# Stick-breaking attention cells: the order of the next cell's scores and logarithms against this cell's sums and weights

## The reference, cut to what matters

```python
h = rms_norm(x, norm_mix_g); proj = h @ w_in          # 1024 tokens, 7 x 1024 columns
z = einsum('bhqd,bhkd->bhqk', q, k) / sqrt(64)         # 16 heads
causal = key_pos < q_pos
log_1m = where(causal, -softplus(z), 0)
after = cumsum(log_1m, reverse=True) - log_1m          # over the keys behind this one
w = where(causal, exp(log_sigmoid(z) + after), 0)
o = w @ v
```

## Time and profile before

| what | value |
|---|---|
| time, median of 3 runs | 4964.03 us (4961.4 to 4964.75) |
| the profiled execution | 4961.57 us, of which its span 4959.8 us |
| PE busy | 4612.5 us, 93% |
| DVE busy | 2884.2 us, 58% |
| ACT busy | 1703.9 us, 34% |
| POOL busy | 1781.3 us, 36% |
| granted TensorE clock, mean | 0.964 of full |
| mixer phase | from the start to 1159.0 us |

### The profile page before, as it was taken

One profiled execution on the slowest core, in us unless ns is written; L12 is line 12 of the kernel. 1 busy time (PEld: TensorE's weight loads), 2 busy tenths in 40 slices (PEclk: granted clock), 3 DMA queues, 4 the chain that ended last, 5 costly groups with the idle time before them and its releaser, 6 DMA issues. The chain is left out here.

```text
span 4959.8 us, 62173 instructions
## 1 busy us (share of the span) xinstructions
PE 4612.5 (93%) x21768; PEld 3671.5 (74%) x21768; DVE 2884.2 (58%) x4467; ACT 1703.9 (34%) x2690; POOL 1781.3 (36%) x1078
## 2 busy tenths in 40 slices
PE   6999999986896987999999998999799999999998
PEld 5666666653676765888888887888688888888886
DVE  3777777776425217777777746776344444444445
ACT  3555555553524313333333333444112111111212
POOL 1443433341124115777777761111122222222221
PEclk9999999987998998999999999999899999999999
DMA  2111111103423131222222224555744444444441
GB/s 78 35 47 48 47 44 43 47 18 128 153 97 132 34 127 69 99 97 93 98 97 93 104 106 144 205 204 210 275 149 134 148 145 144 144 148 145 138 144 68
DMA packets 260002, 555.58 MB, mean 112 GB/s; under 512 B 17104, under 2 KB 148432, under 8 KB 246736
## 3 DMA queue, kind: packets, MB, share of 16 engines
q1 hardware_dynamic: 255184, 485.85, 29.1%
q10 hardware_dynamic: 4608, 67.11, 3.3%
HBM read 384.08 MB, written 168.82 MB: 111 GB/s over the span
## 5 line engine op out<-in xcount | busy, mean ns | idle before, releaser
L155 PE MATMUL expert_o<-expert_ahi,expert_vhi 128*128 128x512 f32 x2048 | 799.5, 390 | 25.8 <-POOL expert_vlo L2338 20.8
L156 PE MATMUL expert_o<-expert_alo,expert_vhi 128*128 128x512 f32 x2048 | 798.5, 390 | 0.0
L157 PE MATMUL expert_o<-expert_ahi,expert_vlo 128*128 128x512 f32 x2048 | 798.3, 390 | 0.0
L2402 DVE TENSOR_TENSOR expert_acc<-expert_acc,expert_o 128x512 f32<-128x512 f32 x496 | 341.0, 688 | 709.8 <-PE expert_o L157 704.7
L2338 POOL TENSOR_TENSOR expert_vlo<-expert_vraw,expert_vhi 128x1024 fp32r<-128x1024 f32 x128 | 323.3, 2526 | 1055.8 <-ACT expert_vhi L2356 1055.8
L155 PEld LDWEIGHTS expert_o<-expert_ahi,expert_vhi 128*128 128x128 f32 x2048 | 385.4, 188 | 108.1 <-issue 27.2
L156 PEld LDWEIGHTS expert_o<-expert_alo,expert_vhi 128*128 128x128 f32 x2048 | 385.5, 188 | 80.2 <-issue 0.2
L157 PEld LDWEIGHTS expert_o<-expert_ahi,expert_vlo 128*128 128x128 f32 x2048 | 385.5, 188 | 80.2
L155 PE MATMUL mix_gemm<-mix_hhi,mix_w_hi 128*128 128x512 f32 x896 | 373.8, 417 | 20.5 <-POOL mix_w_lo L185 13.5
L2362 ACT ACTIVATE expert_ahi<-expert_act 128x1024 fp32r<-128x1024 f32 x128 | 135.8, 1061 | 730.2 <-DVE expert_act L2392 730.2
L556 DVE SCALAR_TENSOR_TENSOR mix_room<-mix_u,mix_cwj,mix_room 128x1024 f32<-128x1024 f32 x240 | 361.3, 1505 | 6.1 <-DVE mix_u L528 3.2
(11 more groups left out here) (319 smaller groups left out, 9983.4 us busy)
## 6 DMA issues: line engine op xcount, KB each, us to landing
gates<-spread_stage ACTq DMA_DIRECT2D x32, 2048.0 KB, 15.0
expert_act<-gelu_u SPq DMA_DIRECT2D x128, 512.0 KB, 3.4
expert_graw<-gates SPq DMA_DIRECT2D x128, 512.0 KB, 4.6
expert_vraw<-in_peer_v SPq DMA_DIRECT2D x128, 512.0 KB, 6.5
select_raw<-in_select_pairs SPq DMA_DIRECT2D x54, 1024.0 KB, 5.0
gelu_u<-front SPq DMA_DIRECT2D x184, 256.0 KB, 2.0
mix_w_raw<-in_w_mix SPq DMA_DIRECT2D x56, 512.0 KB, 3.7
spread_uraw<-in_peer_u SPq DMA_DIRECT2D x36, 512.0 KB, 4.8
```

The source lines that it names most:

```text
L155: nc.tensor.matmul(out, whi, xhi, start=(first and i == 0), stop=False)
L156: nc.tensor.matmul(out, whi, xlo, start=False, stop=False)
L157: mm = nc.tensor.matmul(out, wlo, xhi, start=False, stop=(last and i == len(terms) - 1))
L2402: nc.vector.tensor_tensor(acc[:, k, h * H:h * H + H], acc[:, k, h * H:h * H + H], ops[:, d, h], ALU.add).then_inc(added, 1)
```

## The change

Three queues of the attention cells are put in another order; no arithmetic is added or taken away.

- ACT: the six instructions of the logarithms become the helper `log_part`. Those of cell 0 of the first pair are issued ahead of the loop; inside cell i the logarithms of cell i + 1 (in cell 11, those of cell 0 of the next pair) stand behind the high part and the evictions of cell i and ahead of its weight.
- PE: the scores of cell i + 1 stand ahead of `add_own`(i).
- DVE: both log sigmoids stand ahead of the low part of head 1; each log sigmoid gets a wait for the log weight of the cell before.

```diff
+            def log_part(n, a):
+
+                for s in range(2):
+                    act.wait_ge(z_done[s], n + 1)
+                    nc.scalar.activation(expz[:, s, a:H], zps[:, s, a:H], ACT.Abs).then_inc(act_step[s], 1)
+                for s in range(2):
+                    act.wait_ge(act_step[s], n * 2 + 1)
+                    act.wait_ge(ls_done[s], n + 1)
+                    nc.scalar.activation(expz[:, s, a:H], expz[:, s, a:H], ACT.Exp, scale=-1.0).then_inc(act_step[s], 1)
+                for s in range(2):
+                    act.wait_ge(act_step[s], n * 2 + 2)
+                    nc.scalar.activation(ln[:, s, a:H], expz[:, s, a:H], ACT.Ln, bias=1.0).then_inc(ln_done[s], 1)
+
+            log_part(0, col0[0])
+
             def body(j, par, jj, more):
                 for i in range(NCELL):
                     a, n = col0[i], NCELL * j + i
-
-                    for s in range(2):
-                        act.wait_ge(z_done[s], n + 1)
-                        nc.scalar.activation(expz[:, s, a:H], zps[:, s, a:H], ACT.Abs).then_inc(act_step[s], 1)
...
                     for s in range(2):
                         act.wait_ge(sp_done[s], n + 1)
                         act.wait_ge(sp_used[s], n + 1)
@@ -480,6 +484,8 @@
                     if more and i:
                         for g in ends[i - 1]:
                             evict(*following(j, par, jj), g, more)
+                    if more or i < NCELL - 1:
+                        log_part(n + 1, col0[(i + 1) % NCELL])
                     for s in range(2):
                         act.wait_ge(lw_done[s], n + 1 + 1)
                         act.wait_ge(pv_done[s], n + 1)
@@ -571,11 +577,11 @@
                                                              in1=ln[:, s, a:H], op0=ALU.max, op1=ALU.add)
                         ins.then_inc(sp_raw[s] if masked[i] else sp_done[s], 1)
                     for s in range(2):
+                        dve.wait_ge(lw_done[s], n + 1)
                         nc.vector.scalar_tensor_tensor(out=ls[:, s, a:H], in0=zps[:, s, a:H], scalar=0.0,
                                                        in1=ln[:, s, a:H], op0=ALU.min, op1=ALU.subtract
                                                        ).then_inc(ls_done[s], 1)
-                        if s == 0:
-                            low_part(dve, nc.vector, j, 1, i)
+                    low_part(dve, nc.vector, j, 1, i)
@@ -679,12 +685,12 @@
                 for i in range(NCELL):
                     for s in range(2):
-                        add_own(j, s, i)
-                    for s in range(2):
                         if i < NCELL - 1:
                             z_cell(j, par, s, i + 1)
                         elif more:
                             z_cell(j + 1, 1 - par, s, 0)
+                    for s in range(2):
+                        add_own(j, s, i)
```

## The result

The changed kernel takes 4900.12 us (median, 4897.5 to 4906.8), the kernel before beside it 4962.72 us: a ratio of 0.9877, 95% interval 0.986 to 0.9894. That is 61 us less by the ratio, 63 us by the two medians. The forecast was 4936.6 us with a range of 4922 to 4952: the sign was right, but the gain was more than twice the 27.4 us of the forecast, and the time lies outside the range.

A forecast was written before the change was run, and what follows sets the result against it. PE bounds the first seven pairs, a cell's chain, mostly on DVE, the last. 16.2 + 0.9 + 1.7 (into the last pair) + 7.0 - 1.4 + 3.0 = 27.4 us saved: 4936.6 us, range 4922 to 4952.

The forecast's parts named there:

- The changes of pairs: From cell 11 to the next cell 0, the projection starts 2.7 us earlier; six changes give 16.2 us.
- the clock's 3.0: Behind changes of pairs, less half-rate time on PE: 3.0 us, a quarter of the 12 us possible.
- rival (a): At shortened changes of pairs the clock stays up: 12 instead of 3 us, 4928 us in all; chance 15%.
- The start: At the start of the first pair only the scores gain, 0.9 us, as POOL is at a weight chunk.
- The last pair: Cells of the last pair lose DVE waits for logarithm and high part: 7.0 us saved, bounds 0 and 11.6.
- DVE's new wait for the sums: In the last pair, DVE's log weight waits for sums now behind the next scores: 0.3 to 1.1 us.
- Inside the seven pairs: From cell 8 to 9 the sums end 0.2 us later in each of seven pairs: 1.4 us lost.
- (b): Late masked softplus of cell 0 halves the gain, 1.3 us a change of pairs: 4952 us, halfway 4945; chance 19%.
- (c): PE's wait at changes of pairs only moves, only scores gain, last pair nothing: 4958 us; chance 9%.
- (d): In cells 8 and 9 PE waits for the weight behind the logarithms: slower, 5002 or 4970 us; chance 7%.

The follow-up runs named there:

- The kernel with the held tap: The changed kernel, with DVE's first tap of cell 9 made to wait for POOL's low part of the weight chunk: 4921.43 us, ratio 0.9928.
- D: DVE's part of the change (both log sigmoids ahead of the low part); alone on the kernel before: 4940.47 us, ratio 0.9964.
- S: PE's part of the change (next cell's scores ahead of this cell's sums); alone on the kernel before: 5005.56 us, ratio 1.0092.
- L: ACT's part of the change (next cell's logarithms ahead of this cell's weight); alone on the kernel before: 4965.74 us, ratio 1.0013.

## Why the prediction was right or wrong

The changes of pairs: the sum is right, 22.7 us (21.2 from sums to sums) for 16.2 + 3.0, but two errors cancel in it. PE's wait became 1.04 us (said: about 1) inside the loop's body. These three changes and the one that leaves the loop gained 4.6, 5.2, 5.3 and 4.0 us, 19.0 together, where 4 x 2.7 and the clock's 3.0 were forecast. The clock behind all four was 1.00 where it had been 0.50, so rival (a) holds there. The two over the loop's end gained 2.3 and 1.4 us, not 2.7, with the clock at 0.50 still. The wait there is 2.88 us (said: about 3), but that agreement is luck: I had expected what is left of the wait for POOL's low part, and it is PE's own loop handling ahead of the scores, which the longer chain must have hidden before. The rule of the Trainium skill, "TensorE: Matmul & The Clock Gate", section "HAM oscillation — how this bites in real kernels", that a restart after too long an idle time begins cold, fits both: 1.04 us of waiting left the clock up, 2.88 us did not.

The start: 0.9 us was said, and -1.3 measured, of which 1.1 us had come about before the first scores. That is no mark of the change. The kernel with the held tap has the same code up to there, and its first `weigh` starts at 144.79 us, against 147.00 in the changed kernel and 145.75 before. This term is smaller than what two executions differ by.

The last pair: right in sum, 7.3 (7.8 from sums to sums) for 7.0. From softplus to softplus, the measure of the prediction, cells 8, 9 and 10 took 8.08, 8.51 and 8.02 us instead of 9.46 (said: 8.5 to 9.3 for cells 8 and 9, and 1.9 saved in cell 10). DVE's new wait for the sums, 3.6 us in nine waits over the pair, was nothing in cell 8, 0.25 us in cell 9 and 1.07 in cell 10; I had put 0.3 to 1.1 into cells 8 and 9.

Inside the seven pairs: this step failed, by 29 us: -1.4 was said, and it was 20.0 + 7.7. I walked cell 8 to 9 with "a tap that took 3.45 us beside a weight chunk's low part on POOL" as if 3.45 us were the tap's own length, and took only what the scores would add ahead of it. Its own length is 1.27 us; the rest was waiting behind an operation that had started in the same moment. I had used the rule two paragraphs earlier, for the two low parts of the last pair, that did not run beside each other, and had even found that D ends that meeting 0.6 us sooner. Carried to cell 9, those 0.6 us decide a tie. The Trainium skill states the rule outright, in "SBUF — State Buffer", section "SBUF: two separate sides": whichever of the two starts first, a VectorE operation with two SBUF inputs or a GpSimd operation that reads SBUF, gets the shared port pair for its whole instruction. Its section "Who interferes with whom" adds: "Issue order, not op shape, decides who blocks." The rows before and after agree (3.45 and 1.27 us for the same tap); I had not weighed that page. By the runs 2.6 us of cell 9 are D's in a pair of the loop (3.9 in the first), and D alone gives 17.2 of the 20.0 us in cells 9 and 10.

The 7.7 us of cells 1 to 8, which I had put at nothing, come from S, the order of PE. Between the starts of `weigh`, S alone has the same lengths as the changed kernel in cells 1, 2 and 4 to 8, 0.14 to 0.22 us shorter than before (cell 2: 11.45 us for 11.67), while D alone and L alone leave all of these as they were. PE does not wait for another engine there: with the sums next to the projection, both take 0.1 us less, 1.03 us for 1.12 and 2.80 for 2.90 up to `add_rest`. Why that is so stays open. Cell 3 got 0.3 us longer. The 2.8 us left in cells 9 and 10 are about as much as 0.2 us in each of these 14 cells; no run isolates them.

I had also walked all seven pairs as one. The pairs in the earlier trace rows took 132 and 133 us, but the seventh took 128.3, for the most part because POOL has no chunk beside the tap of its cell 9 (9.47 us for 11.66). That difference stood in the trace of before.

The rivals. (a) came true where PE's wait fell to 1.04 us. (b) and (c) did not: the high part follows the output copies at once, and the last pair gained. (d) did not come where I looked for it (one wait of 0.33 us, in cell 8 of the last pair), but its mechanism is real, as L alone shows. A trace of it is left in the changed kernel: PE waits 0.44 to 0.53 us for ACT's weight in cell 11 of each of the seven pairs, and its waits for POOL's mask of the weight in the last pair grew from 3.6 to 8.3 us, where DVE sets the pace. What I had not said at all is that the three parts hold each other up; I had priced the sum of the parts at each place as if the order of the others were given, and for the kernel as a whole this did no harm.

The time of the later phases differs by 3.9 us between the two profiled executions, against the change: 3804.7 us for 3800.9. Their code is the same, and in eight of the other profiled executions they took 3795.3 to 3801.8 us, so nothing speaks for the change as its cause. The median of the changed kernel lies 6.7 us under its profiled execution.

## What to carry to other kernels

Where an operation shows two lengths in a trace, find what ran beside the long one and ask which started first: half a microsecond on either engine may turn a long one short, here 1.3 against 3.45 us and with PE's wait 2.6 us a pair. A reorder over several engines is priced as a whole: take each part alone, and what waits behind a moved instruction's own input or output bank shows which other part it needs. A wait that goes can be worth more than its length where the clock falls behind it: here PE's wait of 2.30 us was worth 2.6 us.

## What the runs showed of the hardware

DVE's tap (two SBUF inputs, 1.27 us alone) and POOL's low part (2.36 us alone) do not run at once in any of these rows: started together, the tap ended 1.09 us behind the chunk's end; 0.6 us ahead, the chunk took 2.93 = 2.36 + 0.57. DVE's log weight, which has one input in PSUM, took its 1.27 us for two beside the same chunk, as the same page of the Trainium skill has it in "Who interferes with whom": a VectorE instruction with at most one SBUF input does not contend with GpSimd, outside the modes that use both port pairs.

The end of the hardware loop cost 4.9 us of this phase each time (9.8 us for two). In cell 11 it is 2.8 and 2.4 us (8.63 and 8.25 for 5.85), which fits the idle time of 2.88 us on PE and 2.43 on ACT in the rows above; these two run side by side. The rest is in the cell 0 behind it, where the clock is at 0.50 for some microseconds and is at 1.00 when the loop is written out.
